# Final layer norm of a mixture-of-experts decoder step: sums, weights, mean and deviation taken through TensorE and PSUM instead of whole-row VectorE passes

## The reference, cut to what matters

```python
def _layer_norm(x, g, b):
    xf = x.astype(F32)
    mu = xf.mean(-1, keepdims=True)
    var = jnp.square(xf - mu).mean(-1, keepdims=True)
    return ((xf - mu) * lax.rsqrt(var + LN_EPS) * g + b).astype(x.dtype)
...
def _post_block(x, feats, w_o, ln1_g, ln1_b, moe, ln2_g, ln2_b):
    h = _layer_norm(DEEPNORM_ALPHA * x + feats @ w_o, ln1_g, ln1_b)
    return _layer_norm(DEEPNORM_ALPHA * h + _hmoe(h, *moe), ln2_g, ln2_b)
...
        hb = jax.nn.silu(xb @ w_gate[e]) * (xb @ w_up[e])
        return hb @ w_down[e]
```

## Time and profile before

| | |
|---|---|
| median of 3 runs | 1741.7 us |
| the profiled execution's own time | 1740.22 us |
| its span on the core | 1738.4 us |
| TensorE matmul busy | 1499.7 us (86%) |
| VectorE busy | 589.3 us (34%) |
| ScalarE busy | 271.0 us (16%) |
| moved by DMA | 597.36 MB, mean 344 GB/s |

### The profile page before, as it was taken

One profiled execution on the slowest core, in us unless ns is written; L12 is line 12 of the kernel. 1 busy time (PEld: TensorE's weight loads), 2 busy tenths in 40 slices (PEclk: granted clock), 3 DMA queues, 4 the chain that ended last, 5 costly groups with the idle time before them and its releaser, 6 DMA issues.

```text
span 1738.4 us, 24705 instructions
## 1 busy us (share of the span) xinstructions
PE 1499.7 (86%) x10694; PEld 890.0 (51%) x10694; DVE 589.3 (34%) x1268; ACT 271.0 (16%) x619; POOL 73.4 (4%) x88
## 2 busy tenths in 40 slices
PE   7999999999699999998688698976989688787784
PEld 6888788888577577733232233322433333333231
DVE  2845558668363111182321021210212102120126
ACT  0023210120353100021101112110111011111111
POOL 1220011012010000000000000000000000000000
PEclk9999999999797899998887799887999779888887
DMA  9975477777899897329999999999999999999992
GB/s 345 355 275 184 165 264 266 244 259 256 312 364 355 315 299 292 145 114 422 426 425 428 426 416 398 427 425 425 383 427 425 428 425 426 426 425 426 426 422 79
DMA packets 155163, 597.36 MB, mean 344 GB/s; under 512 B 9056, under 2 KB 115232, under 8 KB 121760
## 3 DMA queue, kind: packets, MB, share of 16 engines
q1 hardware_dynamic: 137296, 500.78, 72.9%
q0 software_dynamic: 9792, 75.57, 11.1%
q10 hardware_dynamic: 7960, 19.37, 2.9%
HBM read 586.62 MB, written 17.48 MB: 348 GB/s over the span
## 4 chain that ended last, share of the span: by engine, by line
PE 33%; DMA 28%; DVE 3%; ACT 1%; issue 0%; SPq 0%; DVEq 0%
DMA arena<-in_w_up 28%; PE ps L1930 9%; PE ps L1872 7%; PE ps L1903 6%; PE ps L1962 5%; PE ps L1953 4%; PE ps L1910 1%; ACT arena L1496 1%; PE ps L1832 1%; PE ps L1863 0%; DVE arena L1819 0%; DVE arena L1825 0%; DVE arena L1826 0%; DVE arena L1815 0%; PE ps L1861 0%
## 5 line engine op out<-in xcount | busy, mean ns | idle before, releaser
L1930 PE MATMUL ps<-arena 128*32 128x256 f32 x4352 | 317.2, 448 | 164.0 <-DMA arena<-in_w_up 162.4
L657 PE MATMUL ps<-arena 128*128 128x264 f32 x1664 | 382.6, 388 | 12.0 <-DMA arena<-in_w_in 12.0
L657 PEld LDWEIGHTS ps<-arena 128*128 128x128 f32 x1664 | 313.9, 191 | 64.6 <-issue 12.8
L1930 PEld LDWEIGHTS ps<-arena 128*32 128x32 f32 x4352 | 179.7, 128 | 306.1 <-issue 250.9
L1731 DVE TENSOR_TENSOR arena<-arena,ps 64x256 f32<-64x256 f32 x34 | 14.4, 425 | 526.6 <-ACT arena L1500 526.6
L1903 PE MATMUL ps<-arena 128*32 128x512 f32 (+1 forms) x816 | 188.6, 1028 | 0.0
L1953 PE MATMUL ps<-arena 128*32 128x512 f32 x1088 | 157.6, 683 | 0.0
L1872 PE MATMUL ps<-arena 128*128 128x264 f32 x512 | 121.9, 396 | 1.4 <-PEq L2076 1.4
L1513 ACT COPY arena<-ps 32x512 f32<-32x512 f32 x136 | 78.3, 576 | 251.4 <-PE ps L1953 250.2
L1872 PEld LDWEIGHTS ps<-arena 128*128 128x128 f32 x512 | 97.5, 193 | 24.1 <-issue 7.8
L1962 PE MATMUL ps<-arena,keep 128*128 128x512 f32 (+3 forms) x216 | 101.9, 627 | 1.1 <-issue 1.1
(11 more groups left out here) (416 smaller groups left out, 1058.2 us busy)
## 6 DMA issues: line engine op xcount, KB each, us to landing
arena<-in_w_gate SPq DMA_DIRECT2D x60, 2048.0 KB, 29.5
arena<-in_w_up SPq DMA_DIRECT2D x60, 2048.0 KB, 32.5
arena<-in_w_down SPq DMA_DIRECT2D x60, 2048.0 KB, 32.1
arena<-in_w_in SPq DMA_DIRECT2D x52, 1024.0 KB, 9.2
arena<-in_w_o SPq DMA_DIRECT2D x16, 1024.0 KB, 10.9
arena<-in_w_down SPq DMA_DIRECT2D x8, 1024.0 KB, 30.9
arena<-in_w_up SPq DMA_DIRECT2D x8, 1024.0 KB, 28.3
arena<-in_w_gate SPq DMA_DIRECT2D x8, 1024.0 KB, 32.4
```

The source lines that it names most:

```text
L657: last = pe.matmul(ps[:, n % 2, 0:T], ring[:, slot, k, cols], x[:, k, :], start=(k == 0), stop=(k == KT - 1))
L1930: last = pe.matmul(ps[BS * q:BS * q + BS, 0, 0:CHUNK // 2], xs[:, kk * 4 + i, :], ring[:, s, at:at + CHUNK // 2], start=(k == 0), stop=(k ...
```

## The change

The end of phase_m is written anew, and some of the loop with it.

- ln1_g and ln1_b come as single rows, from the GpSimd queue (8 transfers of 2 KB). In blocks 0 to 3, behind `down`, TensorE spreads a chunk of each over all partitions by a product with one row of ones (`spread`), and `residual` reads them from PSUM, a chunk at a time. ln2_g and ln2_b come as 4 x 32 partitions (8 transfers of 64 KB) from the same queue, once `residual` is done. The four broadcast loads of ln1 and the two of ln2 go.
- The 8 sample tokens' four units become one (four products in four column groups into one bank, `acc_s`), so `n_units` is 9.
- Block 32's part of the ninth group is combined inside `hidden` of block 33, three units ahead of each of its second, third and fourth quarter. Its gates are turned ahead of `hidden`, those of block 33 too, repeated in four row groups (`repeat_gates`, `sel_q`).
- Ahead of the last `down`, `spread_gain` puts the four chunks of ln2_g into PSUM banks, and VectorE makes copies of the running sums with the gain (`with_gain`, `scaled`).
- The number of overflow blocks is loaded in block 6 (HOIST). The test for overflow stays behind the last `down`. The five products with no use go.
- Behind the last `down`, ScalarE copies its result `yq` once. TensorE makes, for each of 2 token tiles and 4 chunks, the sum in PSUM (`summed`: the running sum through the identity, plus block 33's rows by a product over 32 rows), and VectorE takes the statistics there. It makes a second sum with the gain in it (`scaled_sum`), and adds minus mean times gain, and deviation times bias, by two products over one row each (`affine`); mean and deviation were turned to rows by two products (`rows_of`). A last pass of ScalarE or VectorE multiplies each chunk by the reciprocal of the deviation (`scaled_half`).

```diff
+GAIN_BANK = (2, 3, 5, 6)
+SUM_BANK = ((0, 7, 1, 4), (3, 5, 6, 0))
+SCALED_BANK = ((7, 1, 3, 5), (6, 0, 7, 1))
+ROWS_BANK, SAMPLE_BANK = 4, 2
+HOIST = 6
...
-    n_units = 12
+    n_units = 9
...
-            for k, name in enumerate(("ln2_g", "ln2_b")):
-                sp.wait_ge(S["used"], n_wo + 12 * NE + k - NSLOT + 1)
-                sp.dma_start(ln2[k], a[name].broadcast_to([P, D])).then_inc(S["f_ln"], 16)
...
+        @block.gpsimd
+        def _(pool):
+            pool.wait_ge(S["d_ln_free"], 1)
+            for j, name in enumerate(("ln1_g", "ln1_b")):
+                for c in range(4):
+                    pool.dma_start(ln_rows[BS * c:BS * c + 1, j, :], a[name][:, c * CHUNK:(c + 1) * CHUNK]).then_inc(S["d_ln"], 16)
+            pool.wait_ge(S["d_ln_free"], 5)
+            for j, name in enumerate(("ln2_g", "ln2_b")):
+                for c in range(4):
+                    pool.dma_start(ln_rows[BS * c:BS * c + BS, j, :], a[name][:, c * CHUNK:(c + 1) * CHUNK].broadcast_to([BS, CHUNK])
+                                   ).then_inc(S["f_lnq"], 16)
...
-                    for j, name in enumerate(("ln1_g", "ln1_b")):
-                        act.dma_start(ln1[:, j, :], a[name][:, b // 2 * D // 2:(b // 2 + 1) * D // 2].broadcast_to([P, D // 2])).then_inc(S["d_ln"], 16)
...
+                if b == final:
+                    act.wait_ge(S["d_turn"], N_GROUP)
+                    A.copy(sel_t[0:BS, 0:T], ps[0:BS, 5, 0:T])
+                    A.copy(sel_q[:, 0:T], ps[:, 6, 0:T]).then_inc(S["d_turned"], 1)
...
+            act.wait_ge(*down_done(final))
+            A.copy(yq, ps[:, 4, :]).then_inc(S["f_y"], 1)
...
+            def columns(t):
+                act.wait_ge(S["f_mv"], t + 1)
+                if t:
+                    act.wait_ge(S["f_rep"], t)
+                A.activation(column[:, 0], agg[:, t, 0:1].broadcast_to([P, P]), ACT.Copy).then_inc(S["f_w"], 1)
+                A.activation(column[:, 1], agg[:, t, 1:2].broadcast_to([P, P]), ACT.Sqrt, bias=r_("eps")).then_inc(S["f_std"], 1)
...
-                    done.link(v.scalar_tensor_tensor(out[:, half], h[0:n, t, half], ALPHA, ln1[0:n, 0], ALU.mult, ALU.mult))
-                    last = v.scalar_tensor_tensor(out[:, half], ln1[R, 1], ALPHA, out[:, half], ALU.mult, ALU.add)
+                    done.link(v.scalar_tensor_tensor(out, h[0:n, t, chunk], ALPHA, ps[0:n, 6, :], ALU.mult, ALU.mult))
+                    last = v.scalar_tensor_tensor(out, ps[R, 7, :], ALPHA, out, ALU.mult, ALU.add)
...
-                done.link(v.reciprocal(rstd[R, t:t + 1], rstd[R, t:t + 1]))
-                done.link(v.scalar_tensor_tensor(out, out, agg[R, t, 0:1], ln2[0][R, :], ALU.subtract, ALU.mult))
-                v.scalar_tensor_tensor(out, out, rstd[R, t:t + 1], ln2[1][R, :], ALU.mult, ALU.add).then_inc(S["f_o"], 1)
+            def stats_of(t):
+                for c in range(4):
+                    v.wait_ge(S["f_x"], 5 * t + c + 1)
+                    v.bn_stats(fin[:, t, c, :], ps[:, SUM_BANK[t][c], :]).then_inc(S["f_stat"], 1)
...
+            def spread(c):
+                pe.wait_ge(S["d_ln"], 128)
+                if c:
+                    pe.wait_ge(S["d_ln_free"], c + 1)
+                row = slice(BS * c, BS * c + 1)
+                for j in (0, 1):
+                    last = pe.matmul(ps[:, 6 + j, :], r_("ones")[row, :], ln_rows[row, j, :], start=True, stop=True)
+                last.then_inc(S["d_spread"], 1)
...
-            spare_products(5)
...
+            def own_rows(bank, t, c, y, stop):
+                rows = slice(BS * c, BS * c + BS)
+                t0, n = TOK[t]
+                return pe.matmul(ps[:, bank, :], sel_q[rows, t0:t0 + n], y[rows, :], start=False, stop=stop)
+
+            def summed(t, c):
+                pe.matmul(ps[:, SUM_BANK[t][c], :], ident, sums_y[:, t, c * CHUNK:(c + 1) * CHUNK], start=True, stop=False)
+                own_rows(SUM_BANK[t][c], t, c, yq, True).then_inc(S["f_x"], 1)
+
+            def scaled_sum(t, c):
+                pe.matmul(ps[:, SCALED_BANK[t][c], :], ident, scaled[t][:, c * CHUNK:(c + 1) * CHUNK], start=True, stop=False)
+                own_rows(SCALED_BANK[t][c], t, c, yq_g, False)
...
+            def affine(t, c):
+                row = slice(BS * c, BS * c + 1)
+                pe.matmul(ps[:, SCALED_BANK[t][c], :], as_row[row, 0, :], less_g[row, :], start=False, stop=False)
+                pe.matmul(ps[:, SCALED_BANK[t][c], :], as_row[row, 1, :], ln_rows[row, 1, :], start=False, stop=True).then_inc(S["f_sum"], 1)
```

447 lines of the change are left out of this document (310 added, 137 removed).

## The result

The changed kernel takes 1774.3 us (median of 4, 1769.25 to 1778.69), the kernel before in the same comparison 1737.8 (median of 4, 1728.66 to 1746.68): ratio 1.021, 95% interval 1.0145 to 1.0274. It is slower by 2.1%, clear of the interval, and lies outside the range that was forecast (1738 to 1768). The profiled execution took 1775.65 us with a span of 1773.9, so 35.4 more than the profiled one of before.

What follows compares the result with a forecast made beforehand. Weights bind the expert stage, TensorE the end: last `down` at 1697.2 - 8.8 + 8.1 = 1696.5 us, 48.3 of TensorE to 1744.8, last pass and store to 1749.6, forecast 1752 us, range 1738 to 1768.

Steps and rivals of the forecast that it cites:

- Part 4: Behind the last `down`: TensorE is the bound with 48.3 us of work; the stretch grows from 41.2 to 53.1 us.
- the clock as a rival: From the first `affine` on, one-row products and the stop for rows halve the clock: +13 us, 1765 us; chance 0.17.
- The count of passes: TensorE behind the last `down`: 34 passes at 0.86 us, 29.2 us, `affine` 12, changes of row group 5.4.
- Part 3: TensorE from 1656.1 us to the last `down`: edits there add 8.1 us, and weights are no longer waited for.
- Parts 1 and 2: Expert stage: fewer load bytes gain 3.7 us, nine units for twelve gain 5.1; weights arrive 8.8 us earlier.
- the weights are not earlier: Rival: the front's wait or a starving queue eats the 8.8 us gain, 1760 us; chance 0.10.
- The front's wait: At the first `spread`, TensorE waits for eight small row loads: taken as 0, up to 3 us.
- The ln2 rows: Expert stage: 8 loads of 64 KB, counted with 16 KB of ln1 rows as 0.54 MB, 1.3 us of DMA.
- The wide positions: Two places where the weight queue runs dry, losing 3.8 and 4.3 us; each shrinks by 2.6, gain 5.1.
- Small row groups hidden under full passes: Rival: in the end `own_rows` and `affine` run beside identity passes, saving 30 us, 1722 us; chance 0.07.
- Free changes: Rival: changes of row group cost 0 instead of 5.4 + 1.2 us, wide positions give 8.1: 1742 us; chance 0.08.
- the last sum: End of the span at 1749.6 us, 1.8 around it giving 1751.4, median 1.5 above: given as 1752 us.

Runs made afterwards that it cites:

- e3: The changed kernel without the 16 products of `affine`: 1763.9 us.
- e1: The changed kernel with the products of `affine` over 32 rows instead of one: 1771.7 us.
- e5: The changed kernel with its end reordered: a tile's identity products first, then its four 32-row products on four row groups, one-row products likewise in fours: 1741.0 us.
- e2: e1 with block 33's products in the end over all 128 rows instead of 32, which changes the computation: 1746.3 us.
- e6: e5 with the spread of the ln1 rows one block later, behind `hidden`, and `residual` behind `turned`: 1736.8 us.
- e11: e5 with the gain spread by products over 32 rows in place of one row: 1738.3 us.
- e14: The changed kernel with its end's products in pairs, two identity products, then two over 32 rows in neighbouring row groups: 1747.8 us.
- e13: e9 with the two ln2 broadcasts issued after the first combination product of the end instead of right behind the last weights: 1723.4 us, ratio 0.9899.
- e10: e8 with the spread of the ln1 rows back where the changed kernel has it: 1730.7 us, ratio 0.9957.
- e8: The changed kernel's loop with later ln1 spread, and most of the end of the kernel before, without its useless products: 1730.2 us, ratio 0.9947.
- e9: e8 with each of the last two blocks copied once into four row groups and their products four abreast: 1727.7 us.

## Why the prediction was wrong

1. **The step that failed is Part 4's silent assumption of full clock behind the last `down`: every pass was counted at 0.86 us.** The runs showed 0.50 from 1729.1 on, and 18.2 us for it. I had the clock as a rival, with a chance of 0.17 and a price of 13 us from the first `affine` on. The place was right to 1 us (the first `affine` starts at 1728.2), but partly by luck: without `affine` it falls at the same place (e3). The wait for the rows, which the rival named beside it, isn't ruled out. The argument against the rival, that the last group's passes over 64 rows ran at full pace, didn't bear on products over 32 rows that alternate with full ones, and the argument for it named the wrong products (e1, e3). The price by the trace: between 1731.9 and 1762.7 most steps are 2.00 instead of 1.055 us (four one-row products 1.71 instead of 0.86), 30.8 x (1 - 1.055/2.00) = 14.6; the last eight one-row products 3.8 instead of 2.0 (e5), 1.8; the one-row products and the rows in between, 4 us at half speed, about 1.8. Sum 18.2. Without it the end would be, as an estimate, 71.0 - 18.2 = 52.8 us; the forecast was 53.1. The last `down` lost 1.7 more by the clock (5.31 instead of 3.57).

2. **The count of passes was right in sum, by errors that cancel.** A full product and one over 32 rows cost 2 x 1.055 = 2.11 us, against 2 x 0.86 + 0.3 = 2.02 in the sum; the one-row products on four row groups overlap wholly (2.0 us for eight), against 4.3 for five passes. TensorE was the bound, and neither VectorE nor ScalarE came late, as forecast. But 50 passes in this order aren't what the end needs: e5 does the same in 27 us.

3. **Part 3 was right but for the clock.** +10.1 against +8.1, of which 1.7 is the clock. The last `down` no longer waits for weights.

4. **Parts 1 and 2 were too high.** 4.4 us instead of 8.8, so half of the rival "the weights are not earlier" came true. Three terms were mis-sized. The front's wait, taken as 0 up to 3, was 4.35, and `hidden` behind it ran at 0.50 until 800.7 (9.0 us, where one at full clock takes 7.09), so that the queue dipped at 800: (426-285)/426 x 5 = 1.7 us. The ln2 rows were counted by their bytes, 1.3 us, but while they move the queues show a full share at 384, 335 and 346 GB/s: (42+91+80)/426 x 5 = 2.5 more. The wide positions lose 2.9 + 0.7 + 1.0 = 4.7 us, where 2.9 were forecast and 8.1 stood before. Together 8.8 - 1.7 - 2.5 - 1.8 = 2.8; the remaining gain of 1.6 isn't accounted for, but single streams differ by as much (from the first weights to block 32's it is 883.0 us in the changed kernel and 881.1 in e1, with the same loop).

5. **Rivals.** Small row groups hidden under full passes did not happen: they cost 1.055 each between full ones. They do run beside each other, which I had used only for `spread_gain` and for neighbours in `affine`. Free changes fell too: each step costs 0.2 us (e2), 0.4 there and back, where 0.3 was counted.

6. **A slip in the last sum.** 1751.4 and the 1.5 us of the median make 1752.9, not 1752; it changes nothing here.

In sum the forecast missed by 24.3 us of span: 4.4 by the weights, 2.0 in front of the last `down`, 17.9 behind it.

What stays open: whether the wait for the rows and the narrow products around it are needed for the clock to fall, or the alternation of products over 32 and 128 rows is enough; why it then stays down while TensorE is busy (the runs show with which order it does, not what is measured in the chip); why it comes back in e6, e11 and e14 and not in the changed kernel; what brings the short stretches at half clock ahead of the last `down`; the 2.75 us of gap in e13; and how much of e10's gain is the loop's.

## What to carry to other kernels

Put products over few rows next to each other on different row groups, never one by one between full ones: here the same work took 27 instead of 65 us, of which some 18 are the clock's. Before work moves from VectorE's end to TensorE, count it at half clock too: being busy didn't keep the clock up here. And when a change has parts, run them apart: this one held a gain of 0.4% in its loop and in the sample tokens' form, which its new end hid. Work on 8 of 128 partitions cost VectorE as much as work on all (four statistics 2.46 us on 8 partitions, 2.47 on 128, before); laid over all partitions a quarter as wide, the sample tokens took 2.8 instead of 9.6 us (e8).

## What the runs showed of the hardware that was not expected

- TensorE busy for 33.92 of 34 us at a granted clock of 0.50, and in e8 for 15.51 of 16 us with products over 64 rows. The Trainium skill, TensorE: Matmul & The Clock Gate, Why this matters for your kernels, ties the lower clock to idle gaps between bursts; e8 and e9 agree with that (0.50 behind gaps of 5.05 and 4.96 us), the changed kernel's end, whose longest gap is 0.70 us, does not.
- A product of 512 columns over 32 rows between two over 128: 1.055 us for each of them instead of 0.86. Four over 32 rows on four row groups: 1.07 us together; two: 1.05 (e14, 1702.29 to 1703.34).
- Eight loads of 64 KB by GpSimd in the expert stage cost the weights more than their bytes: three stretches of 5 us moved 335 to 384 instead of 426 GB/s, theirs included.
- Instructions arrive by the DMA engines too: around the gap behind the overflow branch five packets of the instruction queues came in (e9 and e13), and it was 4.96 us with 0.83 MB of other transfers in that stretch and 2.75 us without.
